# A two-model forward pass on one core: attention items five deep instead of three, and constant matrix products at the ends of norms and the openings of stages

## The reference, cut to what matters

```python
def masked_softmax(s, mask):
    p = jax.nn.softmax(jnp.where(mask, s, NEG_INF), axis=-1)
    return jnp.where(mask, p, 0.0)
...
        # layer 1: compressed keys, selected keys, window keys
        sc = jnp.einsum('bgrqd,bngd->bgrqn', qb, kc).astype(F32) * scale
        pc = masked_softmax(sc, cmp_end[None, :] <= t[:, None])
        oc = jnp.einsum('bgrqn,bngd->bgrqd', pc.astype(vc.dtype), vc)
...
        o = gb[..., 0:1] * oc.astype(F32) + gb[..., 1:2] * os_.astype(F32) + gb[..., 2:3] * ow.astype(F32)
```

## Time and profile before

| | |
|---|---|
| runs | 3501.94 us median of 3 (3500.34 to 3508.61) |
| profiled execution | 3500.28 us, span 3498.5 us |
| PE busy | 3126.0 us, 89% of the span |
| DVE, ACT, POOL busy | 72%, 52%, 11% |
| attention stage of layer 0 | about 1889.3 to 1926.4 us |
| attention stage of layer 1 | about 2300.8 to 2407.1 us |
| norm stages | 10 run, one more stands in a branch that isn't taken |

### The profile page before, as it was taken

The page is one execution under the profiler, slowest core; times in us unless marked ns, Lnnn a source line. Parts: engine busy times, 40 slices in busy tenths (PEclk is TensorE's granted clock), DMA queues, the critical chain, the costliest instruction groups (busy, mean ns, idle before and its releaser), DMA issues. The chain is left out here.

```text
span 3498.5 us, 67988 instructions
## 1 busy us (share of the span) xinstructions
PE 3126.0 (89%) x27208; PEld 2625.8 (75%) x27208; DVE 2504.4 (72%) x3881; ACT 1802.0 (52%) x3062; POOL 387.2 (11%) x370
## 2 busy tenths in 40 slices
PE   5998888999798898869987899888899999999997
PEld 3774457877673787759975898656789888988996
DVE  4867674449666445577857677566699999999997
ACT  2433233323313665435424444445588888878875
POOL 0000013431000221018300111000000000000000
PEclk8999889999899999979987999868899999999998
DMA  6530033428131000048730798300699999999995
GB/s 233 154 99 1 1 120 122 150 91 298 48 100 24 4 5 4 24 156 272 274 120 25 252 324 303 96 31 26 220 359 376 352 367 351 376 359 360 374 352 197
DMA packets 269600, 647.19 MB, mean 185 GB/s; under 512 B 25453, under 2 KB 123865, under 8 KB 269081
## 3 DMA queue, kind: packets, MB, share of 16 engines
q1 hardware_dynamic: 248457, 567.86, 45.7%
q0 software_dynamic: 20160, 73.41, 5.8%
q10 hardware_dynamic: 720, 2.23, 0.2%
HBM read 642.39 MB, written 1.05 MB: 184 GB/s over the span
## 5 line engine op out<-in xcount | busy, mean ns | idle before, releaser
L4435 DVE TENSOR_TENSOR weights_lo<-raw_ring,weights_hi 128x896 fp32r<-128x896 f32 (+1 forms) x376 | 413.3, 1126 | 50.7 <-ACT weights_hi L4388 40.9
L4388 ACT ACTIVATE weights_hi<-raw_ring 128x896 fp32r<-128x896 f32 (+1 forms) x376 | 366.9, 986 | 90.7 <-PE bank_pair L4358 89.3
L4358 PE MATMUL bank_pair<-weights_hi,expert_x_hi 128*128 128x448 f32 x1024 | 294.7, 369 | 5.1 <-DVE weights_lo L4435 5.1
L4358 PE MATMUL bank_pair<-weights_hi,expert_x_lo 128*128 128x448 f32 x1024 | 292.6, 367 | 0.0
L4358 PE MATMUL bank_pair<-weights_lo,expert_x_hi 128*128 128x448 f32 x1024 | 292.3, 367 | 0.0
L4435 DVE TENSOR_TENSOR weights_lo<-H,weights_hi 128x896 fp32r<-128x896 f32 (+1 forms) x240 | 264.5, 1133 | 23.6 <-ACT weights_hi L4388 14.7
L4388 ACT ACTIVATE weights_hi<-H 128x896 fp32r<-128x896 f32 (+1 forms) x240 | 236.8, 990 | 68.8 <-PE bank_pair L4358 68.8
L2652 DVE SCALAR_TENSOR_TENSOR conv<-bank_pair,vec,conv 128x189 f32<-128x189 f32 (+3 forms) x396 | 138.5, 428 | 146.5 <-ACT conv L2612 146.5
L4358 PEld LDWEIGHTS bank_pair<-weights_hi,expert_x_hi 128*128 128x128 f32 x1024 | 189.9, 188 | 21.4 <-issue 5.0
L4358 PEld LDWEIGHTS bank_pair<-weights_lo,expert_x_hi 128*128 128x128 f32 x1024 | 192.8, 188 | 16.6
L4358 PEld LDWEIGHTS bank_pair<-weights_hi,expert_x_lo 128*128 128x128 f32 x1024 | 192.9, 188 | 16.5
(11 more groups left out here) (798 smaller groups left out, 8302.0 us busy)
## 6 DMA issues: line engine op xcount, KB each, us to landing
raw_ring<-in_moe_w_gate SPq DMA_DIRECT2D x72, 896.0 KB, 6.9
raw_ring<-in_moe_w_up SPq DMA_DIRECT2D x64, 896.0 KB, 7.0
ring_up<-in_ffn_w_up SPq DMA_DIRECT2D x110, 512.0 KB, 4.3
raw_ring<-in_moe_w_down SPq DMA_DIRECT2D x48, 1024.0 KB, 7.3
mod_ring_ada<-in_w_ada POOLq DMA_DIRECT2D x84, 512.0 KB, 6.4
H<-in_moe_w_up SPq DMA_DIRECT2D x48, 896.0 KB, 7.1
ring_down<-in_ffn_w_down SPq DMA_DIRECT2D x66, 512.0 KB, 6.3
H<-in_moe_w_down SPq DMA_DIRECT2D x32, 1024.0 KB, 7.1
```

Of the source, the lines that this page charges most:

```text
L4358: ins = nc.tensor.matmul(banks[half][:, 0:b - a], x, w[:, a:b], start=start and i == 0, stop=stop and i == 2)
L4388: nc.scalar.activation(hi[:, u % CUTS, 0:n].bitcast(F32R), raw_part(u), ACT.Copy).then_inc(cut.sem, 1)
L4435: nc.vector.tensor_tensor(lo[:, u % CUTS, 0:n].bitcast(F32R), raw_part(u)[:, 0:n], hi[:, u % CUTS, 0:n], ALU.subtract).then_inc(parted.sem, 1)
```

## The change

In attention the buffer `scores` gets 5 slots instead of 3 and `low` and `total` get 4 instead of 2. On PE, turn n of the loop now does `score(n)`, `turn(n - 4)`, `add(n - 5)`. `score(n)` waits for the masking addition of item n - 2 alone (`shifted`), no longer for its maximum too. On DVE `mask` and `norm` are cut into single operations and interleaved: in turn n stand the masked addition of n, the reciprocal of n - 2, the maximum of n, then gate, 0/1 mask and scaling of n - 2. On ACT `copy_out` moves ahead of `expo`. Apart from attention, PE gets matrix products of constants (`keep_busy`, 128x128 by 128x512, float32, into a PSUM bank that nobody reads): 4 or 2 at the end of every norm (4 where it covers all 512 tokens) and one at the opening of every `row_stage`, `ffn_up_stage` and of the `swiglu_stage`.

```diff
+            keep_busy(core, st, 5, jobs[-1].items // 2)
...
+def keep_busy(core, st, bank, n):
...
+    for _ in range(n):
+        core.nc.tensor.matmul(core.bank(bank), st.C("ones"), st.const[:, 0:512], start=True, stop=True)
...
         @block.tensor
         def _(pe):
+            keep_busy(core, st, 7, 1)
             for k in range(K):
                 x.wait(pe, k)
...
-        s = core.sb("scores", [P, 3, 2, LAT], ctx=ctx)
-        low = core.sb("low", [P, 2, 2], ctx=ctx)
-        total = core.sb("total", [P, 2, 2], ctx=ctx)
+        TURN_LAG = 4
+        SLOTS, FACTORS, NORM_LAG = TURN_LAG + 1, 4, 2
+        s = core.sb("scores", [P, SLOTS, 2, LAT], ctx=ctx)
+        low = core.sb("low", [P, FACTORS, 2], ctx=ctx)
+        total = core.sb("total", [P, FACTORS, 2], ctx=ctx)
...
                 if n >= 2:
-                    pe.wait_ge(masked.sem, masked.at(n - 1))
+                    pe.wait_ge(shifted.sem, shifted.at(n - 1))
...
-            for n in range(N + 3):
+            for n in range(N + TURN_LAG + 1):
                 if n < N:
                     score(n)
-                if 0 <= n - 2 < N:
-                    turn(n - 2)
-                if 0 <= n - 3:
-                    add(n - 3)
+                if 0 <= n - TURN_LAG < N:
+                    turn(n - TURN_LAG)
+                if 0 <= n - TURN_LAG - 1:
+                    add(n - TURN_LAG - 1)
...
-            for n in range(N + 1):
+            for n in range(N + NORM_LAG):
                 if n < N:
-                    mask(n)
-                if n:
-                    norm(n - 1)
+                    shift(n)
+                if n >= NORM_LAG:
+                    invert(n - NORM_LAG)
+                if n < N:
+                    lowest(n)
+                if n >= NORM_LAG:
+                    gate(n - NORM_LAG)
+                    norm(n - NORM_LAG)
```

More of the change, by code:

```diff
@@ L3668, in attention_stage @@
         begin_ahead(block, ahead)
-        s = core.sb("scores", [P, 3, 2, LAT], ctx=ctx)
-        low = core.sb("low", [P, 2, 2], ctx=ctx)
-        total = core.sb("total", [P, 2, 2], ctx=ctx)
+        TURN_LAG = 4
[3 more added lines that the diff above has]
+        total = core.sb("total", [P, FACTORS, 2], ctx=ctx)
         pt = core.sb("pt", [P, 2, 4, P], ctx=ctx)
-        names = ("scored", "masked", "exped", "normed", "turned", "pt_ready", "summed", "out_taken")
-        scored, masked, exped, normed, turned, pt_ready, summed, out_taken = (core.counter("at_" + n) for n in names)
-        chain = core.counter("vector_chain")
+        names = ("scored", "shifted", "masked", "exped", "inverted", "gated", "normed", "turned", "pt_ready", "summed", "out_taken", "kept")
+        scored, shifted, masked, exped, inverted, gated, normed, turned, pt_ready, summed, out_taken, kept = (core.counter("at_" + n) for n in names)
+        n_gated = lambda n: sum(branches[i].gate is not None for _, _, i in items[:n])
+        n_kept = lambda n: sum(branches[i].some is not None for _, _, i in items[:n])
         SC = [core.psum[i].rearrange("p (h s) -> p h s", h=2) for i in (0, 1)]
@@ L3698, in turn @@
                     for j, (at, w) in enumerate(branches[i].blocks(b)):
-                        ins = nc.tensor.transpose(TR[n % 2][0:w, (h * 2 + j) * P:(h * 2 + j + 1) * P], s[:, n % 3, h, at:at + w], st.C("ident"))
+                        ins = nc.tensor.transpose(TR[n % 2][0:w, (h * 2 + j) * P:(h * 2 + j + 1) * P], s[:, n % SLOTS, h, at:at + w], st.C("ident"))
                 ins.then_inc(turned.sem, 1)
@@ L3742, in expo, with shift @@
                 act.wait_ge(masked.sem, masked.at(n + 1))
-                if n >= 2:
-                    act.wait_ge(normed.sem, normed.at(n - 1))
+                if n >= FACTORS:
+                    act.wait_ge(normed.sem, normed.at(n - FACTORS + 1))
                 for h in (0, 1):
-                    x = s[:, n % 3, h, 0:branches[i].keys(b)]
-                    ins = nc.scalar.activation(x, x, ACT.Exp, bias=low[:, n % 2, h:h + 1], accum_out=total[:, n % 2, h:h + 1])
+                    x = s[:, n % SLOTS, h, 0:branches[i].keys(b)]
+                    ins = nc.scalar.activation(x, x, ACT.Exp, bias=low[:, n % FACTORS, h:h + 1], accum_out=total[:, n % FACTORS, h:h + 1])
                 ins.then_inc(exped.sem, 1)
-            for n in range(N + 4):
-                if 0 <= n - 2 < N:
-                    copy_turned(n - 2)
+            for n in range(N + TURN_LAG + 2):
+                if 0 <= n - TURN_LAG < N:
+                    copy_turned(n - TURN_LAG)
+                if 0 <= n - TURN_LAG - 2 and (n - TURN_LAG - 2) % B == B - 1:
+                    copy_out((n - TURN_LAG - 2) // B)
                 if n < N:
                     expo(n)
-                if 0 <= n - 4 and (n - 4) % B == B - 1:
-                    copy_out((n - 4) // B)
         @block.vector
         def _(dve):
-            c = Chain(dve, chain)
-            def mask(n):
+            def shift(n):
                 b, hp, i = items[n]
@@ L3765, in mask, with lowest, invert, gate @@
                 K = br.keys(b)
-                x = s[:, n % 3, :, 0:K]
                 dve.wait_ge(scored.sem, scored.at(n + 1))
[L3768 to L3772, removed]
+                if n >= SLOTS:
+                    dve.wait_ge(turned.sem, turned.at(n - SLOTS + 1))
+                nc.vector.scalar_tensor_tensor(s[:, n % SLOTS, :, 0:K], SC[n % 2][:, :, 0:K], HD ** -0.5, br.neg[:, b, 0:K].unsqueeze(1).to_broadcast([P, 2, K]),
+                                               ALU.mult, ALU.add).then_inc(shifted.sem, 1)
+            def lowest(n):
+                b, hp, i = items[n]
+                dve.wait_ge(shifted.sem, shifted.at(n + 1))
+                nc.vector.tensor_reduce(low[:, n % FACTORS], s[:, n % SLOTS, :, 0:branches[i].keys(b)], AX, ALU.max, negate=True).then_inc(masked.sem, 1)
+            def invert(n):
+                b, hp, i = items[n]
+                br = branches[i]
+                r = total[:, n % FACTORS]
+                dve.wait_ge(exped.sem, exped.at(n + 1))
+                nc.vector.reciprocal(r, r).then_inc(inverted.sem, 1)
+            def gate(n):
+                b, hp, i = items[n]
+                br = branches[i]
+                r = total[:, n % FACTORS]
+                dve.wait_ge(inverted.sem, inverted.at(n + 1))
+                if br.gate is not None:
+                    nc.vector.tensor_tensor(r, r, br.gate[:, b, 2 * hp:2 * hp + 2], ALU.mult).then_inc(gated.sem, 1)
+                if br.some is not None:
+                    K = br.keys(b)
+                    x = s[:, n % SLOTS, :, 0:K]
+                    nc.vector.tensor_tensor(x, x, br.some[:, b, 0:K].unsqueeze(1).to_broadcast([P, 2, K]), ALU.mult).then_inc(kept.sem, 1)
             def norm(n):
```

13 lines of the change are left out of this document (7 added, 6 removed).

## The result

Five executions of the changed kernel had a median of 3477.34 us (3468.17 to 3487.54), five of the kernel before 3505.42 (3500.34 to 3509.11): ratio 0.9924, 95% interval 0.9902 to 0.9945. That is 27 us faster by the ratio, with 19 and 34 as its bounds. The profiled execution took 3477.34 (span 3475.6), 22.9 less span than the one profiled before.

What follows compares the result with a forecast made beforehand. It took PE to bound layer 1's narrow half and DVE's list its wide half at the full level. From 3500.3 us it subtracted 3.5 (layer 0's attention), 10 (layer 1's) and 8 (constants): 3479; own range 3466 to 3490, whole 3466 to 3494.

Steps and rivals of the forecast that it cites:

- Narrow half: Layer 1's attention, first part: PE-bound at 0.50, gaining only at the start; first wide score at about 2342.8 for 2346.62.
- Triples: Layer 1's wide half at the full level: three items on DVE take 5.1 us for 6.20.
- When the level rises: Layer 1's wide half: rise after two and a half triples, attention -10 us; bounds -18 (at once) and +5 (never).
- Stays up: Layer 1's wide half: once risen the level stays, with PE having 4.6 of 5.1 us of work.
- Layer 0: Layer 0's attention: wide items 1.94 us for 2.12 on DVE, stage -3.5 us, bounds -5 and +5.
- Constants, openings: Six stage openings that start low gain 0.7 us each, -4 together; other gains bring the constants to -10 before costs.
- Constants, norm ends: Norm ends: products fit where PE idles, 0 to 0.2 us late; constants cost +2 us in all.
- The norm with rows: Norm where PE turns modulation rows: no idle cover, two products at the full level add 1.3 us.
- The slower one: Rival: PE stays low in both attentions, +5 us each, and constants only cost; 3512 us, chance 0.06.
- the wide half that stays low: Rival: layer 1's wide attention half never reaches the full level; 3494 us, chance 0.18.
- the constants give nothing: Rival: a level raised at an opening falls again in the idle gap of 1 to 2 us; 3489 us, chance 0.13.
- the narrow half that rises: Rival: layer 1's narrow attention half also reaches the full level, -17 us, wide items up at once, -8; 3454, chance 0.05.

Runs made afterwards that it cites:

- depth alone: Kernel before with all constants, five score buffers, turns four items behind and adds five, DVE's order untouched; 0.9949 against the kernel before.
- four deep: Changed kernel with four score buffers and turns three items behind instead of four; 0.996 against the kernel before.
- none behind rows: Changed kernel without constant products at the end of the four norms in which PE also turns modulation rows; 0.9938 against the kernel before.
- three deep: Changed kernel with three score buffers and turns two items behind, as before the change; 1.0309 against the kernel before.
- six first: Changed kernel plus six constant products of 512 columns at the very start of each attention stage; 0.9974 against the kernel before.
- filler: Changed kernel plus one constant product of 256 columns ahead of each narrow score in attention; 0.997 against the kernel before.

## Why the prediction was right, and where its steps were off

The forecast of 3479 stands 2 us from the median and the time lies in the forecast's own range. Its split fits the kernels with one half of the change: 13.5 for the attention (14 measured alone) and 8 for the constants (6 alone). That it is so close is luck in part. In the profile after, layer 1's attention gave 16.7 us for 10, layer 0's 1.1 for 3.5, and all other stages together 5.1 for 8: one miss of 6.7 us and two of 5.3 together nearly cancel. Below that the steps differ too.

- **Narrow half: right.** First wide score 41.7 us after the stage's start for 42.0 predicted (2342.8 on the old scale); 0.50 throughout.
- **Triples: right in size, half right in cause.** 5.19 for 5.1. I took all of the gain from DVE's order. With the depth alone the triple fell from 6.20 to 5.67, and only the last 0.5 is the order's. The prediction had listed the wait for a score (0.44) without asking what removes it. The order without the depth is 108 us slower, a slower rival that wasn't among mine: the prediction treated the depth as given and never asked what the order needs of it.
- **When the level rises: wrong in size, in favour.** "Two and a half triples" would be some 72 us after the stage's start. Behind the first wide score it rose after 3.5 to 4.1 us in five kernels with five deep and the new order (at 45.5 in the whole change), and after 15.6 (at 57.3) in the one with constants at the openings alone. With the rise at 57.3 the attention lasted 92.5, with 45.5 it was 89.6; by that slope a rise at 72 gives 96.0 (an estimate), which is where I had put the end. So the late rise alone can account for the miss. My "at once" bound (-18) was the nearer one, at -16.7. The reason I gave fails: with four deep the level stood at 0.50 for 19.7 us in which full-width pieces came three in a row without a gap, and with five deep it rose behind two wide scores. Depth, order and moment can be told apart by stages with nearly the same rise, one profile each. Constants alone (rise at 59.1) 105.2, depth alone (59.2) 95.7, whole attention change (57.3) 92.5, the same at 45.5 89.6: 9.5 by depth, 3.2 by DVE's order, 2.9 by the moment. The 9.5 holds a fall too: with the constants alone the level dropped again at 79.6, for 6.8 us, and at 100.1 to the end, with the depth it stayed up.
- **Stays up: right.** 1.00 from 2344.9 to 2385.9. This is a part of the gain that neither 6.20 nor 5.1 shows: in the profile before the level fell at 67.5, 81.1, 94.8 and 101.6 us after the stage's start, and behind its rise the triples took 6.20 and 7.50 in turn.
- **Layer 0: the pace right, the sum not.** DVE does an item in 1.92 (predicted 1.94):

```profile
1912.98 0.69 DVE L3781 SCALAR_TENSOR_TENSOR scores<-bank_pair,keep 128x512 f32<-128x512 f32 x1
...
1914.90 0.68 DVE L3781 SCALAR_TENSOR_TENSOR scores<-bank_pair,keep 128x512 f32<-128x512 f32 x1
```

  But only the last few items run so. The stage went from 37.1 to 36.0, not to 33.6, as the level rose 24.6 us into it, before 21.6. In the kernel without constants it rose at 18.7, and the stage took 34.3.
- **Constants, openings: right in direction, mixed in size.** Window behind the opening of the row stage of the earlier trace rows, after:

```profile
1922.80:1925.80 3.00, 2.25 (x12) 1.48 (x13) 2.26 (x5) 2.96 (x7) 0.00 (x0) 1.00 0.00 0
```

  1.00 from the start, and the stage takes 26.62 for 28.01: 1.4, where I took 0.7. It is 26.62 or 26.63 in all kernels with a constant there, 27.97 in the one changed kernel without. The other openings are less clean: the ten stages with a constant at theirs are 5.9 us shorter together in the profile after, from -2.3 to +1.3 each, for the 8.5 that I added up. The ten norm stages are 3.9 longer together, and the stages that hold no edit 3.1 shorter.
- **Constants, norm ends: hidden as said.** Of the ten norm stages seven changed by less than 0.25 us in the profile after, one by +0.3, one by -0.8; the tenth is the next point.
- **The norm with rows: mis-sized.** I had +1.3, from two products at the full level, and it was +3.9. In time order, after:

```profile
2174.72 3.43 PE L1128 MATMUL bank_pair<-const 128*128 128x512 f32 x4
...
2175.14 0.24 DVE L752 SCALAR_TENSOR_TENSOR next_coef<-next_mod,vec 128x8 f32<-128x8 f32 x2
```

  The products took 3.43, nearly all at the low level, and DVE was done at 2175.38, 14.7 us into the stage. In the two kernels where the level moved in the same way and no product stood there (no constants at all; none behind rows) DVE was done 14.7 us in as well, and the stage lasted 14.9. So 2.8 of the 3.9 are the products', the other 1.2 the level's. With the same two products and the level down for fewer us (three deep) the stage had +0.9 in all, with the level down throughout (six first) +6.8. The price of a constant depends on the level at which it runs, and so does everything around it; leaving these out gained nothing measurable.
- **Rivals.** The slower one is out, as both attentions got shorter; the wide half that stays low was seen in part (four deep); "the constants give nothing" is out by 0.9982 (0.9971 to 0.9993); the narrow half that rises came only with a filler, and gave nothing, as the filler took what the level gave: 1.74 us an item (2315.41 to 2331.05, nine items) for 1.9.

The Trainium skill ("TensorE: Matmul & The Clock Gate", Part 1: The HAM clock gate) ties the level to how busy the engine was. The traces don't bear that out for this stage by busy time alone: in both windows of the filler PE was busy throughout, at 0.50 in one and at 1.00 in the other. The same section says that one kernel can have more or fewer slow matmuls from run to run (it gives 6, 11 and 14). The traces agree that it varies, but the size is another here: the two rises of one program lay 62 us apart, at 11.2 and 72.9 us after the stage's start.

What stays open: what in a stream of pieces decides the level, and when. Without a filler or constants the narrow half stayed at 0.50 in every profile, but its pieces differ from the wide ones in more than their columns, a third of all pieces are transposes, and no run separates these. Two products of 512 columns ahead of the wide half had the level up by at most 0.5 us after their end, in both layers of both kernels that had them. In layer 1 with five deep the level rose as early without them, and with four deep 27 us later, each in one profile.

## What to carry to other kernels

Before one engine's list is reordered to finish an item later, count the ring that it forms with its consumer: with DVE scaling two items behind, PE's turns two behind cost 108 us, three behind left a wait of 0.8 us in each triple, four behind none. Work out a stage's length at both clock levels, since the moment of the rise can be worth as much as the edit. Don't read a change of some us in one stage of one profile as the edit's work: a stage that no edit touched (250 to 436 us before) lasted 185.0 to 190.6 us over these kernels. And ask of a forecast that comes out right whether its terms did. Filler products pay where PE would idle anyway and dense work follows (1.4 us for one product); in a stage that PE bounds they eat what they give.

## What the runs showed of the hardware

- PE busy for all of 39.9 us stayed at 0.50, and in another execution of the same program ran at 1.00 for 35.3.
- A level that six constants had raised at 2316.9 fell again at 2323.7, 3.6 us after the last constant, with PE on narrow pieces and busy for 2.7 of these.
- With four deep PE was busy for all of 19.7 us, with wide pieces three in a row, at 0.50.
- A stage with none of its instructions changed moved with the level: the norm with rows from 13.7 us at a mean of 0.75 to 17.6 at 0.51, with 72 instructions on PE in both.
